# Where modulation units 8 to 15 are worked out: inside the first attention instead of inside its input GEMM

## The reference, cut to what matters

```python
mod = (silu_c @ w_mod[l] + b_mod[l]).reshape(bsz, N_MOD, 1, D_MODEL)
mod_c = (silu_cc @ w_mod[l] + b_mod[l]).reshape(N_MOD, D_MODEL)
sh1, sc1, g1, sh2, sc2, g2 = [mod[:, j] for j in range(N_MOD)]
h = modulate(rmsnorm(x, norm_g[l, 0]), sh1, sc1)
y, yc = even_mixer(h, hc, ...)   # input GEMM, spatial gating, rope, attention, output GEMM
x = x + g1 * rmsnorm(y, norm_g[l, 1])
h = modulate(rmsnorm(x, norm_g[l, 2]), sh2, sc2)
```

## Time and profile before

| | |
|---|---|
| Median of 3 runs | 2079.87 us |
| The profiled execution's own time | 2074.43 us |
| Its span, first to last instruction | 2072.6 us |
| Mean granted TensorE clock | 0.959 of full |
| PE busy | 1936.0 us, 93% of the span |
| DVE busy | 1296.5 us, 63% |
| ACT busy | 1107.2 us, 53% |
| PE L563 in all (units 0 to 47) | 2% of the chain that ended last |

### The profile page before, as it was taken

How to read it: one execution, slowest core, us unless ns; L and a number is a source line. 1 busy time by engine, 2 the same in 40 slices (tenths; PEclk the granted TensorE clock), 3 DMA queues, 4 the chain that set the end, 5 groups by cost and what they waited for, 6 DMA issues and landing times.

```text
span 2072.6 us, 26215 instructions
## 1 busy us (share of the span) xinstructions
PE 1936.0 (93%) x9984; PEld 1542.0 (74%) x9984; DVE 1296.5 (63%) x1261; ACT 1107.2 (53%) x1124; POOL 28.2 (1%) x44
## 2 busy tenths in 40 slices
PE   4998798999999999878899999999999999999996
PEld 3876476888878687348788787887878878788785
DVE  2344726232233541564788888889888898888885
ACT  3423535222223342354477776777777777776773
POOL 0000000000000000210000000000000000000000
PEclk9998999999999999798699999999999999999997
DMA  9453155433222453111699898998989999899991
GB/s 323 137 163 122 59 165 186 140 102 99 84 87 97 138 187 102 21 56 62 223 367 360 309 366 306 362 360 319 360 310 369 343 325 365 304 376 330 332 377 41
DMA packets 263897, 473.34 MB, mean 228 GB/s; under 512 B 17112, under 2 KB 116368, under 8 KB 263824
## 3 DMA queue, kind: packets, MB, share of 16 engines
q1 hardware_dynamic: 262928, 469.31, 64.6%
q0 software_dynamic: 896, 3.02, 0.5%
HBM read 471.25 MB, written 1.05 MB: 228 GB/s over the span
## 4 chain that ended last, share of the span: by engine, by line
PE 81%; DVE 8%; ACT 4%; issue 4%; SPq 1%; DMA 1%; POOL 0%; DVEq 0%; ACTq 0%
PE bank L500 23%; PE bank L502 23%; PE bank L501 23%; PE bank L563 2%; PE bank L1722 2%; DVE split_low L1468 2%; PE bank L708 2%; PE bank L1764 1%; PE bank L683 1%; SPq L876 1%; DVE y L1455 1%; PE bank L698 1%; PE bank L357 1%; PE bank L370 1%; DVE small L767 1%
## 5 line engine op out<-in xcount | busy, mean ns | idle before, releaser
L1468 DVE TENSOR_TENSOR split_low<-raw_weights,split_high 128x2048 fp32r<-128x2048 f32 x224 | 511.7, 2287 | 59.3 <-ACT split_high L1164 58.4
L1164 ACT ACTIVATE split_high<-raw_weights 128x2048 fp32r<-128x2048 f32 x224 | 429.0, 1919 | 147.0 <-PE bank L502 146.9
L484 DVE TENSOR_TENSOR split_low<-raw_weights,split_high 128x1024 fp32r<-128x1024 f32 x118 | 143.9, 1225 | 329.4 <-ACT split_high L479 329.4
L500 PE MATMUL bank<-h_high,split_high 128*128 128x512 f32 (+1 forms) x848 | 324.5, 383 | 21.9 <-DVE h_low L414 9.9
L501 PE MATMUL bank<-h_low,split_high 128*128 128x512 f32 (+1 forms) x848 | 322.3, 380 | 0.0
L502 PE MATMUL bank<-h_high,split_low 128*128 128x512 f32 (+1 forms) x848 | 322.2, 380 | 0.0
L1468 DVE TENSOR_TENSOR h_low<-raw_weights,h_high 128x2048 fp32r<-128x2048 f32 x112 | 256.6, 2291 | 77.9 <-ACT h_high L1164 77.9
L500 PE MATMUL bank<-split_high,xe_high 128*128 128x512 f32 x672 | 271.9, 405 | 14.6 <-DVE split_low L1468 14.6
L502 PE MATMUL bank<-split_high,xe_low 128*128 128x512 f32 x672 | 266.2, 396 | 0.0
L501 PE MATMUL bank<-split_low,xe_high 128*128 128x512 f32 x672 | 266.1, 396 | 0.0
L1164 ACT ACTIVATE h_high<-raw_weights 128x2048 fp32r<-128x2048 f32 x112 | 214.8, 1918 | 42.9 <-PE bank L502 42.9
(11 more groups left out here) (241 smaller groups left out, 2665.9 us busy)
## 6 DMA issues: line engine op xcount, KB each, us to landing
raw_weights<-in_moe_w SPq DMA_DIRECT2D x336, 1024.0 KB, 6.8
raw_weights<-in_w_mod SPq DMA_DIRECT2D x48, 1024.0 KB, 5.6
raw_weights<-in_ffn_w SPq DMA_DIRECT2D x33, 1024.0 KB, 5.3
raw_weights<-in_ev_w_in SPq DMA_DIRECT2D x10, 1024.0 KB, 11.8
raw_weights<-in_od_w_in SPq DMA_DIRECT2D x8, 1024.0 KB, 9.3
raw_weights<-in_ev_w_out SPq DMA_DIRECT2D x4, 1024.0 KB, 9.0
raw_weights<-in_od_w_out SPq DMA_DIRECT2D x4, 1024.0 KB, 5.6
overlay<-in_rpb SPq DMA_DIRECT2D x32, 64.0 KB, 2.3
```

The costliest lines, as they stand in the source:

```text
L484: dve.tensor_tensor(half_of(s, j, SPL[:, s % NSPLIT, :]), half_of(s, j, raw_of(split_at[s])), half_of(s, j, SPH[:, s % NSPLIT, :]).bitcast ...
L500: pe.matmul(ps, wh, xh, start=first, stop=False)
L1164: act.activation(esplit(u)[0], RAW[:, u % NRAW, :], ACT.Copy).then_inc(S("e_high"), 1)
L1468: dve.tensor_tensor(lo, RAW[:, u % NRAW, :], hi.bitcast(F32), ALU.subtract)\
```

## The change

- In the list of loads, units 8 to 15 stand after the first output unit, together with 16 to 23 (there were 16 to 20 after the first and 21 to 23 after the second output unit).
- The `pe_mod_rows`, `pe_mod_turn` and `act_mods` calls for units 8 to 15 are gone from the input GEMM and from behind it. The four rope products of units 8 and 9 follow each other directly.
- The values of the first attention all use bank 5. The wait before a pair's values is for DVE's copy of the pair before it (it was for the one before that).
- Bank 6 holds the modulation: one unit's 256 outputs at a time in columns 0 to 255 (`pe_mod_half`), the turned pairs in columns 288 to 319 (`pe_half_turn`). ACT copies each unit by itself (`act_mod_half`, 256 wide, 8 copies where there were 4 of 512).
- PE does unit i + 5 at iterations i = 3 to 10 of its attention loop, after the transposes and before the values, and turns a pair at i = 5, 7, 9 and 11, ahead of that. Unit i waits until ACT has copied all units before it (`half_rows`). ACT copies unit i + 3 at the head of its iterations i = 5 to 12.
- The wait for `mod_evac` 4 before the attention is one for 2; `dve_mods` for units 8 to 15 stands behind DVE's attention, and PE waits for it there.

```diff
@@ -109,12 +109,10 @@
     units += mods(0, 8)
     for s in range(10):
         units.append(("split", "ev", cols(w["ev_w_in"][0], 256 * s)))
-        if s >= 6:
-            units += mods(2 * s - 4, 2 * s - 2)
     for s in range(4):
         units.append(("split", "evo", cols(w["ev_w_out"][0], 256 * s)))
-        if s < 2:
-            units += mods((16, 21)[s], (21, 24)[s])
+        if s < 1:
+            units += mods(8, 24)
     units += mods(24, 28)
     for s in range(FT // 2):
         units += [("split", "up", cols(w["ffn_w1"][0], 256 * s)), ("split", "up", cols(w["ffn_w3"][0], 256 * s))]
@@ -155,7 +153,7 @@
 PBANK = (0, 1, 3, 6)
 CBANK = (6, 7, 2, 3)
 TBANK = (4, 7)
-OBANK = (5, 6)
+OBANK = ((5, 5), (5, 6))
 
 
 def trunk(nc, w, out):
@@ -552,11 +550,15 @@
                         if k == KT - 1:
                             m.then_inc(S("bank_full"), 1)
 
+        def rows_done(g):
+
+            return g if g <= 4 else g - 4
+
         def pe_mod_rows(pe, i, bank):
             r = mod_at[i]
             pe.wait_ge(S(f"raw{r % NRAW}"), need[r])
             if i % 2 == 0 and i >= 2:
-                pe.wait_ge(S("mod_rows"), i // 2)
+                pe.wait_ge(S("mod_rows"), rows_done(i // 2))
             wt = raw_of(r).rearrange("p (k n) -> p k n", k=KT)
             for h in range(2):
                 for j in range(4):
@@ -564,8 +566,36 @@
                                      SC[:, 4 * h + j, :], wt[:, 4 * h + j, :], start=(h == 0), stop=(h == 1))
             last.then_inc(S("mod_used"), 1)
 
+        def pe_mod_half(pe, i):
+
+            r = mod_at[i]
+            pe.wait_ge(S(f"raw{r % NRAW}"), need[r])
+            pe.wait_ge(S("half_rows"), i - 8)
+            wt = raw_of(r).rearrange("p (k n) -> p k n", k=KT)
+            for h in range(2):
+                for j in range(4):
+                    last = pe.matmul(PS[6][32 * j:32 * j + 32, 0:256], SC[:, 4 * h + j, :], wt[:, 4 * h + j, :],
+                                     start=(h == 0), stop=(h == 1))
+            last.then_inc(S("mod_used"), 1)
+
+        def pe_half_turn(pe, g):
+
+            pe.wait_ge(S("half_rows"), 2 * g - 6)
+            for c in range(4):
+                c0 = 256 + 8 * g + 2 * c
+                last = pe.matmul(PS[6][:, c0:c0 + 2], MROW[:, g % 2, P * c:P * c + P], CON[:, C_SEL:C_SEL + 2],
+                                 start=True, stop=True)
+            last.then_inc(S("mod_turned"), 1)
+
+        def act_mod_half(act, i):
+
+            act.wait_ge(S("mod_used"), i + 1)
+            act.wait_ge(S("mod_turned"), i // 2 - 1)
+            c = 256 * (i % 2)
+            act.activation(MROW[:, i // 2 % 2, c:c + 256], PS[6][:, 0:256], ACT.Copy).then_inc(S("half_rows"), 1)
+
         def pe_mod_turn(pe, g, bank):
-            pe.wait_ge(S("mod_rows"), g + 1)
+            pe.wait_ge(S("mod_rows"), rows_done(g + 1))
             for c in range(4):
                 c0 = 8 * (g % 12) + 2 * c
                 last = pe.matmul(PS[bank][:, c0:c0 + 2], MROW[:, g % 2, P * c:P * c + P], CON[:, C_SEL:C_SEL + 2],
@@ -624,9 +654,10 @@
                     act.wait_ge(S("mod_turned"), g - 1)
                 act.activation(MROW[:, g % 2, :], PS[rows][:, :], ACT.Copy).then_inc(S("mod_rows"), 1)
 
-        def dve_mods(dve, v0, v1, bank):
-
-            l, m0, c0, n = v0 // 6, 8 * (v0 % 6), 16 * (v0 % 6), v1 - v0
+        def dve_mods(dve, v0, v1, bank, col=None):
+
+            l, m0, n = v0 // 6, 8 * (v0 % 6), v1 - v0
+            c0 = 16 * (v0 % 6) if col is None else col
             dve.wait_ge(S("mod_turned"), 2 * v1)
             dve.tensor_tensor(MOD[:, l, m0:m0 + 8 * n, :],
                               PS[bank][:, c0:c0 + 16 * n].rearrange("p (m v) -> p m v", v=2),
@@ -668,13 +699,13 @@
 
 
 
-        def pair_out(units, p):
-
-            u = units[2 * p]
+        def pair_out(a, p):
+
+            u = (att0, att1)[a][2 * p]
             t, c = u["dst"]
-            return PS[OBANK[p % 2]][u["o"], :2 * P], (u["o"], t, slice(c, c + 2 * P))
-
-        def pe_attention(pe, a, units):
+            return PS[OBANK[a][p % 2]][u["o"], :2 * P], (u["o"], t, slice(c, c + 2 * P))
+
+        def pe_attention(pe, a, units, between=lambda i: None):
             def scores(i):
                 u = units[i]
                 if i >= 2:
@@ -698,19 +729,21 @@
                         last = pe.transpose(PS[TBANK[(i - 1) % 2]][:, P * kt:P * kt + P],
                                             PB[:, 2 * ((i - 1) % 2), P * kt:P * kt + P], ident)
                     last.then_inc(S(f"ptrans{a}"), 1)
+                between(i)
                 if i >= 3 and i % 2 == 1:
                     p = (i - 2) // 2
                     u = units[2 * p]
                     pe.wait_ge(S(f"pt{a}"), 2 * p + 2)
-                    if p >= 2:
-                        pe.wait_ge(S(f"o_evac{a}"), p - 1)
+                    if p >= 1 + a:
+                        pe.wait_ge(S(f"o_evac{a}"), p - a)
                     for kt in range(u["nk"]):
-                        last = pe.matmul(pair_out(units, p)[0], u["v"][kt], PT[p % 2][:, kt, :],
+                        last = pe.matmul(pair_out(a, p)[0], u["v"][kt], PT[p % 2][:, kt, :],
                                          start=(kt == 0), stop=(kt == u["nk"] - 1))
                     last.then_inc(S(f"o{a}"), 1)
 
-        def act_attention(act, a, units):
+        def act_attention(act, a, units, between=lambda i: None):
             for i in range(len(units) + 3):
+                between(i)
                 if i < len(units):
                     u = units[i]
                     act.wait_ge(S(f"negmax{a}"), i + 1)
@@ -736,7 +769,7 @@
                 if i >= 4 and i % 2 == 0 and a == 1:
                     p = (i - 3) // 2
                     act.wait_ge(S("o1"), p + 1)
-                    src, dst = pair_out(units, p)
+                    src, dst = pair_out(a, p)
                     act.activation(HH[dst], src, ACT.Copy).then_inc(S("o_high"), 1)
 
         def dve_attention(dve, a, units):
@@ -987,8 +1020,6 @@
 
             for g, s in run("ev"):
                 to(g + 1)
-                if s >= 6:
-                    act_mods(act, s - 2, s - 1, 7)
                 for j in range(2):
                     act.wait_ge(*bank_full(g, j))
                     b = PS[j]
@@ -1013,7 +1044,13 @@
             for g in range(4):
                 act.wait_ge(S("sgu_out"), g + 1)
                 act.activation(HH[:, g, :], U[:, g, :], ACT.Copy).then_inc(S("sgu_high"), 1)
-            act_attention(act, 0, att0)
+
+            def halves_between(i):
+
+                if 5 <= i <= 12:
+                    act_mod_half(act, i + 3)
+
+            act_attention(act, 0, att0, halves_between)
 
             act_table(act, ACT.Sqrt, 48)
             act_squares(act, N["sub0"])
@@ -1261,8 +1298,8 @@
                 dve.wait_ge(S("sgu_high"), g + 1)
                 dve.tensor_tensor(HL[:, g, :], U[:, g, :], HH[:, g, :].bitcast(F32), ALU.subtract)\
                    .then_inc(S("mix0"), 1)
-            dve_mods(dve, 2, 4, 6)
             dve_attention(dve, 0, att0)
+            dve_mods(dve, 2, 4, 6, 256 + 32)
             for b in range(2):
                 dve.wait_ge(*norm_root(f"sub{b}"))
                 dve.reciprocal(N[f"sub{b}"]["root"], N[f"sub{b}"]["root"]).then_inc(S("norm_recip"), 1)
@@ -1532,30 +1569,32 @@
             pe_spread(pe, N["n0"])
             for g, s in run("ev"):
                 if s in (6, 7):
-                    pe_mod_rows(pe, 2 * s - 4, 7)
-                    pe_mod_rows(pe, 2 * s - 3, 7)
                     if s == 6:
                         pe.wait_ge(S("sgu_v"), 1)
                         pe.wait_ge(S("wst"), 1)
                     pe_sgu(pe, 2 * s - 12)
                     pe_sgu(pe, 2 * s - 11)
                 if s in (8, 9):
-                    pe_mod_turn(pe, s - 4, 6)
-                    for h in range(2):
-                        pe_rope(pe, 0, lambda i: (S("ev_evac"), 9 + i), range(4 * s - 32 + 2 * h, 4 * s - 30 + 2 * h))
-                        pe_mod_rows(pe, 2 * s - 4 + h, 7)
+                    pe_rope(pe, 0, lambda i: (S("ev_evac"), 9 + i), range(4 * s - 32, 4 * s - 28))
                 if s == 0:
                     gemm_first(pe, [(g, PS[0:2])], 0, "n0_hl")
                     continue
                 kind = "t" if s in (2, 3, 8, 9) else "f"
                 free = [(S("ev_evac"), 2 * s - 1 + j) if s else None for j in range(2)]
                 gemm_unit(pe, g, kind, 0, PS, free)
-            for g in (6, 7):
-                pe_mod_turn(pe, g, 6)
             pe.wait_ge(S("ev_evac"), 20)
             pe.wait_ge(S("roped0"), 8)
+            pe.wait_ge(S("mod_evac"), 2)
+
+            def halves_between(i):
+
+                if i in (5, 7, 9, 11):
+                    pe_half_turn(pe, i // 2 + 2)
+                if 3 <= i <= 10:
+                    pe_mod_half(pe, i + 5)
+
+            pe_attention(pe, 0, att0, halves_between)
```

(1 more changed line is left out.)

## The result

The changed kernel takes 2088.06 us (median of 6 runs, 2086.84 to 2089.44) against 2080.12 for the kernel before (6 runs, 2077.97 to 2082.87): a ratio of 1.0041, 95% interval 1.0029 to 1.0053. It is slower by 8 us. Forecast were 6.3. In the table the first row is a part of the second.

The account below looks back on a forecast made before the run. In the attention the order of PE's instructions was taken to count, its idle time being bound to places. Terms: 13.9 - 5.7 - 1.6 - 0.3 = 6.3 us slower, from 2079.87 to 2086.2 us; range 2080.5 to 2091.0.

Parts of the forecast that it names:

- unit 23's load: After the attention: PE's 0.34 us wait for the load of unit 23 goes, 0.3 us gained.
- the loop PE, ACT, PE becomes the period: Attention: PE waits for ACT's copy after every transpose step from i = 4 to 10, 0.60 or 0.38 us by shape.
- The term of the attention: Transposes of unit 2 to those of unit 12: 41.4 us where it was 27.5, so 13.9 us more.
- I take the high clock from i = 5 on: Attention: PE busy for some 78% in the new loop, so its steps from i = 5 were summed at 2.4 GHz.
- The term of the GEMM: Input GEMM: removed modulation units take 2 x 1.86 + 2 x 1.00 = 5.7 us off the path.
- Before GEMM units 8 and 9, 2 x 1.00: Input GEMM: only the second modulation unit of two is on the chain there, 1.00 us gained each time.
- The join: Between GEMM and attention: DVE goes from `h_low` directly to the first maxima, 1.6 us gained.
- The tail: After unit 12's transposes: 0 up to the first squares' sums, then 0.3 us gained up to the norms' last `h_high`.
- only busy time counts: Rival, attention: PE's idle time takes up 5.0 of 11.9 us added, growth 6.9, total 2079.2 us; chance 0.12.
- DVE stays the period: Rival, attention: added work runs beside DVE, leaving the 7.6 us gained and 1.6 of clock: 2070.7 us; chance 0.06.
- The low clock: Rival, attention: short stops for ACT bring PE to 1.2 GHz from i = 5 to 11, some 20 us more, 2106; chance 0.04.
- the rival of 2.9 us: Attention: values in one bank lay bare a 0.42 us copy for each of 7 pairs, total 2089.1 us; chance 0.08.

Follow-up runs that it names:

- the faster version: Changed kernel with units 8 to 11 in the rope gaps, 12 to 15 ahead of the attention's transposes: 2065.57 us, ratio 0.9934 to the kernel before.

## Why the prediction was right

Direction and size held (8 measured, 6.3 forecast, in the range). Term by term it was less good, and part of the nearness is luck. The two large errors did not cancel: the attention cost 3.9 more than forecast and the GEMM gave 1.7 less, both to the changed kernel's loss. With 0.3 that unit 23's load did not give, and 1.0 gained ahead of the squares, the first pair of traces has 11.1 for 6.3.

What brings that down to the 7.9 of the medians is the kernel before. Its first trace is a short execution, with 16.55 us in the norms where its second trace has 18.70 and the run with the single bank 18.59, at the low clock. The second pair of traces gives 17.5 in the attention, -4.6 in the GEMM, -1.7 at the join, -0.9 ahead of the squares and -2.2 in the norms: 8.2. So 2.2 us of low clock in the norms, in other executions of the kernel before, stood in for what the sum had missed, with 0.8 less in attention and GEMM, and no term of the forecast spoke of them.

**The mechanism was right.** The step "the loop PE, ACT, PE becomes the period" is what the trace shows: waits for ACT's copy in place of the waits for DVE, and DVE idle up to 4.2 us. Removing that wait alone took 7.8 us off, some 1 of it clock, where the steps give 7.0 for the copies. The iterations without a low clock came as summed: 3.34 for i = 6, 8 and 10 (3.3 forecast), 5.49 for 7 (5.2), 6.15 for 9 (6.1).

**The term of the attention was too small by 3.9.** "I take the high clock from i = 5 on" is the step that failed. i = 5 took 7.8 for 6.1 and the last stretch 3.9 for 2.8: 2.8 us. The prediction had allowed for the rest of the clock, but not in its sum: i = 3 took 4.3 for 3.1, i = 4 was 0.9 shorter. That makes 3.1 us net from spells. The other 0.8 is 0.1 to 0.3 more in each of the iterations from 6 to 11, handoffs which I had let cancel. The argument behind the step was a mean (76% busy at a clock of 0.90). The first spell comes right behind an idle time of 1.86 us (198.66), which a mean hides; the second behind one of 0.75 (208.53), and the same 0.75 at 228.48 brings none, so I have no rule to put in the mean's place.

**The term of the GEMM was too large by 1.7.** "Before GEMM units 8 and 9, 2 x 1.00" gave nothing in the first trace: 36.66 against 36.64 us. In the second it gave 0.5, and over the five traces with this GEMM from 0.9 gained to 1.3 lost. At a full clock, with the gaps filled, it gave 2.4. The second units were on the path, but the first ones, priced at nothing because DVE's split covers them, had been keeping the clock up. I named the work that hides them and not what they held up. The Trainium skill (TensorE: Matmul & The Clock Gate, Why this matters for your kernels) says to avoid idle gaps between bursts of matmuls; I weighed it for the attention only, and it bore on the rope gaps, as the run with the filled gaps shows. The units before GEMM units 6 and 7 gave 2.05 each, for 1.86.

**The join** gave 1.66, as forecast. **The tail** had 1.0 less from the clock, unforecast. PE's wait for unit 23's load is gone, as forecast, but the 0.3 did not show (16.53 against 16.55).

**The rivals.** That only busy time counts gave +6.9 for the attention; with the change's order it was 17.8. But with the work ahead of the transposes it was 4.3: my sum was for the change's order, and that order is most of the cost. That DVE stays the period fell for the change, and is what the faster version does: there DVE is busy for 24.4 of 27.2 us. The low clock came in three spells that cost some 4.5 us against the same steps at full clock, and not throughout. The rule of the Trainium skill (Perfetto Trace Analysis, Optimizing Tensor Performance, Matmuls) to rotate independent groups of matmuls through different banks stood beside the rival of 2.9 us; measured was a ratio of 0.9997, so here the order of DVE's work decides and the rule does not bite.

## What to carry to other kernels

Idle time of an engine is room only where it stands: put the added work into the very wait, ahead of the instruction that waits, and not behind it, where it delays what others wait for. Before removing work that is off the path, ask what its being there keeps going; on TensorE, in the rope gaps, that was the clock. Take a second trace before trusting a sum of stages to a microsecond or two: two executions of the kernel before differed by 2.4 us in the stretch of the table, with nothing changed. And where a result must be copied out by an engine with its own order, place the copy so that it is done an iteration before it is asked for.

## What the runs showed of the hardware

Work without a use made a stretch faster: with 16 matmuls of no use in each rope gap, GEMM units 8 and 9 took 34.3 us instead of 36.7 (36.1 in the second trace), at a granted clock of 1.00 instead of 0.50 behind the gaps. And the spells at 1.2 GHz came at the same instructions in the attention of two executions of the changed kernel (1.92 and 1.94 us for its first unit, 1.94 and 1.94 for its third), while in its GEMM the same wait was followed by one in the first execution (2.46 us, then 0.50) and by none in the second (2.45 us, then 1.00), and the attention of the kernel before had its spell at another place in each of two executions (204 to 208 and 215 to 218). What fixes their place was not settled.
